# Moving a TensorE stationary buffer by 64 bytes in SBUF

## What is computed

```
def block(args):
    xb, eb, gb = args
    a = jnp.einsum('nd,nhkd->nhk', xb, jnp.take(u_tab, eb, axis=0))
    w = (gb * jax.nn.gelu(a.astype(jnp.float32))).astype(xb.dtype)
    return jnp.einsum('nhk,nhkd->nd', w, jnp.take(v_tab, eb, axis=0))
```

## The kernel before

| tile | role | first byte | left over 128 |
|---|---|---|---|
| `vw_hi`, before | stationary, blocks 0 to 123 | 223808 | 64 |
| `vw_lo`, before | stationary, blocks 0 to 123 | 225856 | 64 |
| `vw_last_hi`, `vw_last_lo` | stationary, blocks 124 to 127 | 16512, 20608 | 0 |
| `xt_hi`, `xt_lo` | stationary, projections | 98432, 114816 | 0 |
| `w_hi`, `w_lo` | moving, all blocks | 163968, 172160 | 0 |
| `hi`, `raw_lo` | moving, projections | 168064; 131200 and on | 0 |
| `qk_t` | float32 (not float32r), attention scores, L854 | 215616 | 64 |
| `pq_t` | float32 stationary, key scores, L2235 | 41088 | 0 |

## Time and profile before

### The profile page before, as it was taken

How to read it: one execution, slowest core, us unless ns; L and a number is a source line. 1 busy time by engine, 2 the same in 40 slices (tenths; PEclk the granted TensorE clock), 3 DMA queues, 4 the chain that set the end, 5 groups by cost and what they waited for, 6 DMA issues and landing times.

```text
span 3155.3 us, 39929 instructions
## 1 busy us (share of the span) xinstructions
PE 2994.9 (95%) x12354; PEld 2188.0 (69%) x12354; DVE 2373.6 (75%) x4369; ACT 1872.6 (59%) x4178; POOL 307.0 (10%) x372
## 2 busy tenths in 40 slices
PE   8999999999999999988987799899999999999998
PEld 6888888888887888776776233333334888888886
DVE  6788777888868568866858899999997555555556
ACT  5655545555556765454455688787787555555554
POOL 1000000000000000000000333333331000000000
PEclk9999999999999999978999555555556999999999
DMA  7667767777776558940844899999998555555554
GB/s 260 213 213 227 220 235 239 241 245 242 244 244 227 174 173 286 374 167 21 300 135 155 359 413 411 383 405 411 412 421 356 189 188 189 188 187 186 186 186 147
DMA packets 214208, 792.95 MB, mean 251 GB/s; under 512 B 17410, under 2 KB 18130, under 8 KB 151458
## 3 DMA queue, kind: packets, MB, share of 16 engines
q1 hardware_dynamic: 159040, 408.99, 39.9%
q0 software_dynamic: 51344, 370.53, 29.8%
q10 hardware_dynamic: 3668, 11.53, 1.0%
HBM read 783.64 MB, written 7.34 MB: 251 GB/s over the span
## 4 chain that ended last, share of the span: by engine, by line
PE 66%; DVE 18%; DMA 10%; ACT 2%; issue 2%; DVEq 1%; ACTq 1%; POOL 0%; POOLq 0%
PE bank L496 12%; PE bank L498 12%; PE bank L497 12%; DVE u_ring L2569 8%; DMA u_ring<-in_peer_u,idx 8%; PE bank L2745 7%; PE bank L2747 7%; PE bank L2746 7%; DVE u_more L2569 3%; DVE raw_lo L486 1%; DVE acc L551 1%; DMA ada_ring<-in_ada_w 1%; PE bank L854 1%; ACT hi L480 1%; DMA raw<-in_w_in 1%
## 5 line engine op out<-in xcount | busy, mean ns | idle before, releaser
L480 ACT ACTIVATE hi<-raw 128x512 fp32r<-128x512 f32 x1008 | 600.5, 627 | 451.4 <-PE bank L498 252.5
L486 DVE TENSOR_TENSOR raw_lo<-raw,hi 128x512 fp32r<-128x512 f32 x1008 | 658.9, 690 | 254.8 <-ACT hi L480 251.2
L496 PE MATMUL bank<-hi,xt_hi 128*128 128x512 f32 x1632 | 655.8, 402 | 24.5 <-DVE raw_lo L486 24.2
L498 PE MATMUL bank<-hi,xt_lo 128*128 128x512 f32 x1632 | 638.0, 391 | 0.0
L497 PE MATMUL bank<-raw_lo,xt_hi 128*128 128x512 f32 x1632 | 638.0, 391 | 0.0
L2499 PE MATMUL bank<-row_ring,one_row 96*128 96x512 bf16 x1024 | 529.2, 621 | 54.5 <-DVE act_in L2569 25.3
L2668 DVE TENSOR_TENSOR w_lo<-v_raw,w_hi 128x512 fp32r<-128x512 f32 x496 | 343.4, 693 | 292.3 <-ACT w_hi L2641 289.9
L2641 ACT ACTIVATE w_hi<-v_raw 128x512 fp32r<-128x512 f32 x496 | 313.1, 632 | 330.8 <-PE bank L2747 330.8
L2569 DVE CUSTOM_DVE_ANT_0 u_ring<-u_ring,bank 128x1024 f32<-128x1024 f32 x344 | 405.7, 1216 | 29.7 <-DMA u_ring<-in_peer_u,idx 18.0
L2745 PE MATMUL bank<-w_hi,vw_hi 128*128 128x512 f32 x992 | 395.2, 398 | 3.0 <-DVE w_lo L2668 3.0
L2746 PE MATMUL bank<-w_lo,vw_hi 128*128 128x512 f32 x992 | 394.9, 398 | 0.0
(11 more groups left out here) (453 smaller groups left out, 3497.8 us busy)
## 6 DMA issues: line engine op xcount, KB each, us to landing
v_raw<-in_peer_v SPq DMA_DIRECT2D x128, 1024.0 KB, 4.8
ada_ring<-in_ada_w POOLq DMA_DIRECT2D x96, 1024.0 KB, 7.1
raw<-in_w_in_ab SPq DMA_DIRECT2D x128, 512.0 KB, 3.8
raw<-in_w_in_c SPq DMA_DIRECT2D x128, 512.0 KB, 4.0
raw<-in_w_in SPq DMA_DIRECT2D x120, 512.0 KB, 3.7
raw<-in_w_out_ab SPq DMA_DIRECT2D x32, 512.0 KB, 4.3
raw<-in_w_out_c SPq DMA_DIRECT2D x32, 512.0 KB, 4.4
raw<-in_w_out SPq DMA_DIRECT2D x32, 512.0 KB, 6.3
```

The costliest lines, as they stand in the source:

```text
L480: act.activation(hi[:, c % HI, :], raw[d % RAW][:, c % KC, :], ACT.Copy).then_inc(hi_ready, 1)
L486: dve.tensor_tensor(raw_lo[d % RAW][:, c % KC, :], raw[d % RAW][:, c % KC, :], hi[:, c % HI, :].bitcast(F32), ALU.subtract).then_inc(lo_sp ...
L496: pe.matmul(o, a_hi, b_hi, start=kk == 0, stop=False, skip_group_check=True)
L498: last = pe.matmul(o, a_lo, b_hi, start=False, stop=kk == K - 1, skip_group_check=True)
```

## The change

`vw_hi` and `vw_lo` begin 64 bytes further on: at 223872 and 225920, both multiples of 128. Their size, their distance from each other, all instructions, waits and their order stay as they are. The 64 bytes at the end that are newly used belong to a constant area that has no reader in this stage.

```
         assert first_const + 16384 <= m_row1_at
-        vw_hi = at("vw_hi", [P, 2, S], m_row1_at + 8192, F32R)
-        vw_lo = at("vw_lo", [P, 2, S], m_row1_at + 10240, F32R)
-        assert m_row1_at + 12288 <= 229368
+        vw_hi = at("vw_hi", [P, 2, S], m_row1_at + 8192 + 64, F32R)
+        vw_lo = at("vw_lo", [P, 2, S], m_row1_at + 10240 + 64, F32R)
+        assert m_row1_at + 12288 + 64 <= 229368
```

## The result

The changed kernel takes 3137.38 us in the median of 22 runs (3132.21 to 3143.57), the kernel before 3144.08 us in 22 runs (3137.34 to 3153.14). The ratio is 0.9973, with a 95% interval from 0.9965 to 0.9982: 6.7 us less by the medians (0.21%), 0.27% by the ratio. I had forecast 19.8 us less. The time lies inside the stated range, the direction is right, and the size is a third of what I said. The range holds it only because I had stretched it from the forecast's own 3116 to 3132 us up to the case of no change. By the bound of 0.3% the result belongs to "no change", although its interval lies wholly under 1.

What follows compares the result with a forecast made beforehand. PE alone was taken to pace blocks 0 to 123; 2966 steps by 6.67 ns less gave -19.8 us, other terms nothing, so 3143.62 - 19.8 = 3123.8 us. Range 3115 to 3144 us, the forecast's own 3116 to 3132.

Steps and rivals of the forecast that it cites:

- no change: Rival: pitch in blocks 0 to 123 stays at 233.3 ns, time 3143.6 us; chance 0.15.
- What bounds the stage: Blocks 0 to 123: PE alone paces them, busy 688.00 of 688.00 us, so time saved there comes off the end.
- The stationary tiles' address is what differs: Blocks 0 to 123: stationary tiles at remainder 64 over 128 cost 6.67 ns more per matmul than remainder 0 elsewhere.
- The term of the sum: PE in blocks 0 to 123: 2966 steps at full clock, each falling from 233.33 to 226.67 ns, give -19.8 us.
- Carrying the difference over to the median: Whole kernel: profiled execution stood 13.5 us above the median; the same -19.8 us was taken from the median, 3143.62.
- The writes: ACT's and DVE's copies into the stationary tiles: +1 and -2 ns by 248 instructions each, under 0.5 us, beside PE's work.
- the ring: Chunk buffering ahead of PE: three chunks, 4.08 us, cover 2.49 us of ACT and DVE work, so PE does not wait.
- DMA: Block loads: 1 MB every 5.44 us instead of 5.60, 196 GB/s, below the projection's 243; no cost.
- the waits: Value product stage: PE has no wait; ACT's wait for PE becomes smaller by 40 ns each time.
- Slower: two reads that meet: Rival: equal remainders make stationary and moving reads meet; pitch 240 ns, +19.8 us, 3163.4 us; chance 0.04.
- The pitch of the columns alone: Rival of more gain: blocks 0 to 123 fall to 213.5 ns, -59 us, 3084.8 us; chance 0.02.
- Part of the gain: Rival: only two of three steps, those with a new stationary, gain; -13.2 us, 3130.4 us; within the forecast's 0.79.

Runs made afterwards that it cites:

- b_moving64: Kernel before with the moving tiles w_hi and w_lo (and two v_raw buffers) moved 64 bytes, stationary tiles left alone: 3158.53 us, ratio 1.0038.
- c_plus192: Kernel before with vw_hi and vw_lo moved by 192 bytes: 3155.67 us, ratio 1.0029.
- d_both: Kernel before with vw_hi and vw_lo moved by 128 bytes and w_hi, w_lo (and two v_raw buffers) by 64: 3138.86 us, ratio 0.9973.
- a kernels: Kernel before and changed kernel, each rerun unchanged and with the matmuls of blocks 0 to 123 issued twice, on one chip; before beside them 3143.7 us.
- a_before_again: The kernel before, unchanged, profiled and timed once more: 3140.11 us, ratio 0.9998.
- d kernels: d_both, kernel before with vw_hi and vw_lo moved by 96 bytes, and the changed kernel again; before beside them 3146.8 us.
- b_plus128: Kernel before with vw_hi and vw_lo moved by 128 bytes, moving tiles left alone: 3156.48 us, ratio 1.0035.

## Why the prediction was right or wrong

**What bounds the stage: right.** PE paces it, before and after, and the changes of pitch came out in the time by the number of steps, within the noise (b_moving64 has some 4 us more than its pitch accounts for).

**The stationary tiles' address is what differs: right, but by the wrong measure.** I took the remainder over 128. c_plus192 refutes it. What the pitch follows is the difference between stationary and moving tile over 256. The change sets it to 0 as well as the remainder I had named, so that the changed profile came out as foretold. That was luck: a move by 192 bytes would have met my rule just as well, and the kernel would have been slower. I had struck the moving tiles off the list because they are the same memory in the slow and in the fast place, which says nothing on how the two addresses stand to each other. My observation that the new address "leaves 128 over 512", as the fast tiles do, was nearer to it than the rule I argued from, and I didn't ask what the moving tiles had.

**The term of the sum: the step that failed.** 2966 steps by 6.67 ns. The steps and the 226.7 are right; the 233.33 of before is the pitch of a rare execution. Most have 228.9, so the term is 2966 x 2.2 = 6.6 us instead of 19.8, and 3144.1 - 6.6 = 3137.5 is the time measured. Of 126 timed executions of before beside these experiments and in the result, 16 are above 3150 us, and of 54 of the changed kernel and d_both, at 226.7 ns in their profiles, none is above 3144. That these 16 are the executions at 233.3 ns is argued from their time alone; they have no trace, and what lies outside the stage varies too (by the traces it took between 2454 and 2468 us, a spread as large as the effect), so the share of the slow rhythm is rough. It is not steady either: none of 23 beside the a kernels (but one of the 11 of a_before_again, at 3160.4 us), 6 of 25 beside the d kernels on the same chip.

**Carrying the difference over to the median: where it could have been seen.** The profiled execution of before was 13.5 us above the median of its runs, and I treated that as an offset that cancels. It was the effect itself: 2966 x 4.4 = 13.2 us of it is the slow rhythm, and what lay outside the stage, 2458.9 us, was near the middle of the profiles (2457.3). The other profile of the same program, a_before_again, took 3148.57 us, 8.5 above its own runs' median, with the stage at 683.6 and 2463.1 us outside it, so not every excess of a profile is of this kind; but an excess as large as the gain forecast needed an explanation before the gain was counted.

**The writes, the ring, DMA, the waits: right.** Nothing came late. ACT and DVE take what they took, and PE has no wait in the stage.

**The rivals.** "No change" gave 3143.6 by a pitch that stays; the pitch moved, and yet the time, 3137.4, came out nearer to that than to the 3123.8 of the forecast. "Slower: two reads that meet" is wrong in its sign: equal places are the fast ones. But its idea, that stationary and moving address act together, is the right one, and I had used the projections against it when they speak for it. The pitch of the columns alone, 213.5 ns, was never seen. "Part of the gain" wanted some steps of the changed kernel to stay slow; none did. What is partial is the loss before, in the mixed rhythm: of steps of 226, 229 and 232 ns, one in three loses nothing.

**The rules of the skill.** By the Trainium skill, page "SBUF — State Buffer", section "Door 1: The DMA port swizzle", lines of 16 bytes are what SBUF has, and crossing from line to line costs. The runs moved tiles by whole lines, between 32 and 256 bytes, and pitches from 226.7 to 233.3 ns came of it, so that rule does not describe this. By the Trainium skill, page "TensorE: Matmul & The Clock Gate", section "Step-by-step: what each phase is for", moving and stationary operand have read ports of their own, and loading the next weights takes no bandwidth from the running matmul. In d_both against b_plus128 the moving tiles have moved and the stationary ones have not, and the pitch is 226.7 ns instead of 233.3 (3138.9 us instead of 3156.5, on different chips; ratios to the kernel before of 0.9973 and 1.0035). So here the two operands are not independent.

**What stays open.** Why one of the two rhythms takes hold at difference -64, why the two parts act together, and by what mechanism the difference acts at all: the runs show that the pitch follows it, and that a shift by 128 bytes changes the pitch while one by 256 does not, but not what in the chip has that period. Differences that are not multiples of 32 were not tried, and `w_hi` and `w_lo` always had the same remainder.

## What to carry to other kernels

Give the stationary and the moving tiles of a stream of float32r matmuls the same remainder over 256 bytes; here that was worth 1 to 3% of the stream (226.7 ns against 228.9 and 233.3), and cost nothing. When a profiled execution stands above the median of its runs by as much as the gain you expect, compare the pitch in a second profile before you price anything with it. A trait that two fast places share is only a candidate: vary it through other values before you call it the cause.

## What was not expected of the hardware

A stream of equal matmuls at full clock can lock into one of two rhythms at one and the same address (233.3 ns, or 226, 229 and 232 in turn) and hold it for some 2960 steps. One disturbance in 123 moved it into the slow one, the next one out of it. A shift by 32 bytes moves the pitch of 512-column float32r matmuls from 226.7 to 233.3 ns (3%), and the last four blocks got slower, 226.7 to 228.9, when the tiles that were moved were the moving ones alone.
